# Residuals scaled and stored in the second mixer's opening, router tables first, and a page norm inside the pooling

## The reference, cut to what matters

```
for l in (0, 1):
    mixer = gated linear attention + SSD scan         if l == 0
            causal pooling + block-sparse attention   if l == 1     # paged K/V cache for the sample rows
    x = LayerNorm(alpha * x + mixer(x) @ w_out, ln_g[l, 0], ln_b[l, 0])      # alpha = 4 ** 0.25
    x = LayerNorm(alpha * x + experts(x),       ln_g[l, 1], ln_b[l, 1])      # 32 experts, 2 per row

def _layer_norm(x, g, b):
    return (x - mean(x)) * rsqrt(var(x) + LN_EPS) * g + b
def _pool_mix(u, buf, ...):   # s = sum of the last w rows, w = 2, 4, 8, 16 for four groups of 128 columns
    outs.append((s / cnt - u[..., lo:hi]) @ w_pool[group])
def _hier_moe(x, ...):        # router: 4 coarse + 32 fine logits of x; top group, then the top 2 experts of it
    ... silu(x @ w_gate) * (x @ w_up) * gate @ w_down
```

## Time and profile before

| what | value |
|---|---|
| median of 3 runs | 1218.51 us (1217.38 to 1221.27) |
| the profiled execution | 1223.9 us, its span 1222.1 us |
| PE busy | 1106.7 us (91%) |
| DVE busy | 501.2 us (41%) |
| ACT, POOL busy | 234.3 us (19%), 178.5 us (15%) |
| mean DMA rate over the span | 294 GB/s |

### The profile page before, as it was taken

How to read it: one execution, slowest core, us unless ns; L and a number is a source line. 1 busy time by engine, 2 the same in 40 slices (tenths; PEclk the granted TensorE clock), 3 DMA queues, 4 the chain that set the end, 5 groups by cost and what they waited for, 6 DMA issues and landing times. The chain is left out here.

```text
span 1222.1 us, 15209 instructions
## 1 busy us (share of the span) xinstructions
PE 1106.7 (91%) x5759; PEld 558.9 (46%) x5759; DVE 501.2 (41%) x1363; ACT 234.3 (19%) x519; POOL 178.5 (15%) x177
## 2 busy tenths in 40 slices
PE   8999999989999988876899999989899999788892
PEld 6874666655553333222543345544555433222330
DVE  3614666567642211111532314654787421111116
ACT  0311223321121100000421212333111211000003
POOL 0000000000011111100535532320000111111023
PEclk9999999999999999899999999989898999899895
DMA  7520210439489999996979979894895899999975
GB/s 289 191 97 4 78 67 1 147 119 422 179 309 408 420 420 420 420 421 249 394 281 328 381 264 365 299 363 174 325 378 199 319 408 419 419 421 421 421 284 222
DMA packets 85099, 358.84 MB, mean 294 GB/s; under 512 B 13959, under 2 KB 18188, under 8 KB 55324
## 3 DMA queue, kind: packets, MB, share of 16 engines
q1 hardware_dynamic: 63420, 279.57, 57.6%
q0 software_dynamic: 19520, 74.01, 15.7%
q10 hardware_dynamic: 2080, 4.19, 0.9%
HBM read 342.75 MB, written 31.16 MB: 306 GB/s over the span
## 5 line engine op out<-in xcount | busy, mean ns | idle before, releaser
L1896 PE MATMUL ahead_psum<-m_wg,top_xT 128*64 128x512 f32 x704 | 201.0, 633 | 33.2 <-DMA m_wg<-in_moe_w_gate_up 26.4
L1896 PEld LDWEIGHTS ahead_psum<-m_wg,top_xT 128*64 128x64 f32 x704 | 60.9, 145 | 145.9 <-issue 103.4
L1921 PE MATMUL n_psum_m<-m_wd,top_xT 128*64 128x512 f32 x456 | 121.1, 601 | 1.6 <-ACT top_xT L1979 1.0
L1896 PE MATMUL ahead_psum<-top_wide,top_xT 128*64 128x512 f32 x288 | 99.6, 624 | 12.5 <-DMA top_wide<-in_moe_w_gate_up 7.6
L1378 PE MATMUL ahead_psum<-top_wide,top_xT 128*128 128x512 f32 x224 | 103.0, 605 | 1.5 <-PEq L159 1.5
L1961 DVE COPY top_xT<-n_psum_t 128x512 f32<-128x512 f32 x31 | 21.4, 692 | 177.7 <-PE n_psum_t L1881 177.7
L2348 PE MATMUL ahead_psum<-top_wide,top_xT 128*128 128x512 f32 x192 | 86.0, 596 | 3.8 <-issue 3.3
L1816 POOL DMA_INDIRECT expert_rows<-e_Y,m_dest x33 | 32.9, 996 | 371.9 <-DVE e_Y L1970 334.2
L2152 POOL DMA_INDIRECT cd_kv<-in_cache_kT,top_kpages x64 | 61.0, 954 | 56.1 <-PE cd_psum_d L2391 32.4
L1378 PEld LDWEIGHTS ahead_psum<-top_wide,top_xT 128*128 128x128 f32 x224 | 41.1, 193 | 44.4 <-issue 44.3
L1921 PEld LDWEIGHTS n_psum_m<-m_wd,top_xT 128*64 128x64 f32 x456 | 35.3, 137 | 56.0 <-issue 53.2
(11 more groups left out here) (521 smaller groups left out, 1701.5 us busy)
## 6 DMA issues: line engine op xcount, KB each, us to landing
m_wg<-in_moe_w_gate_up SPq DMA_DIRECT2D x96, 1024.0 KB, 27.1
m_wd<-in_moe_w_down SPq DMA_DIRECT2D x56, 1024.0 KB, 26.8
top_wide<-in_moe_w_gate_up SPq DMA_DIRECT2D x32, 1024.0 KB, 20.3
cd_kv<-in_cache_kT SPq DMA_DIRECT2D x64, 256.0 KB
top_X<-in_moe_w_down SPq DMA_DIRECT2D x8, 1024.0 KB, 28.0
ab_w<-in_ab_w_in SPq DMA_DIRECT2D x2, 2048.0 KB, 11.2
top_wide<-in_ab_w_in SPq DMA_DIRECT2D x2, 2048.0 KB, 7.8
top_wide<-in_ab_w_out SPq DMA_DIRECT2D x2, 2048.0 KB, 8.9
```

The lines of the kernel that those rows point to most:

```text
L1896: last = nc.tensor.matmul(pg[i % 2][64 * a:64 * a + 64, :], xgT[i % 2][:, j, 64 * a:64 * a + 64], wg[E.slot(i, a)][:, j * 512:(j + 1) * 51 ...
L1921: last = nc.tensor.matmul(py[n2][64 * a:64 * a + 64, :], hT[:, j, 64 * a:64 * a + 64], wd[E.slot(i, a)][:, j * D + n2 * 512:j * D + (n2 + ...
```

## The change

1. In the second mixer's opening SP also loads gain and bias of `ln[0, 1]`, spread over 128 partitions, into the memory of the tile `vt`, between the expert rows and the weights of the projection. DVE's `restore(i)` stands there now, its five calls between `normal_scale(4)` and `copy_scores(1)`. SP stores each tile after its `restore` and no longer after ACT's norm. Its list is now: page group 0, tile 4, page group 1, tiles 0 and 1, group 2, tiles 2 and 3, group 3 and on. The memset of Q is moved behind `rotate("q", 0)`; the copy of the page scores waits for two stored tiles at group 0 and for the other two at group 4; ACT writes `vt` only after the last `restore`.
2. In the settling of l = 1 `restore` and its loads are gone. The router's three loads are the first that SP issues. DVE's list begins with the blanks and the tables. PE's `prepare()` stands between the two halves of tile 0 instead of behind a half of tile 1.
3. In the settling of l = 0 `prepare()` stands in the middle of the second half of `project(1, 1)`. In both layers `prepare_out()` is ahead of `add(1, 1)` on DVE.
4. In `window(3)` DVE runs `p_norm(7)` when sums of width 4 are made, instead of after the window and the copy of `newS`.

```diff
@@ settle_parts, sync
+        router()
         if back:
-            for i, (t, P) in enumerate(ORDER):
+            for t, P in ORDER:
                 sp.dma_start(X[:P, t, :], back(t)).then_inc(x_in[t], 16)
-                if i == 0:
-                    for p, got in ((slice(0, 32), old_in), (slice(32, 128), rest_in)):
-                        for a in range(2):
-                            sp.dma_start(E.xg[a][p, :], old[a].partition_broadcast(p.stop - p.start)).then_inc(got, 16)
-                        if got is old_in:
-                            router()
...
@@ settle_parts, tensor
             project(1, 0, second)
+            prepare()
             project(1, 1, second)
...
-            project(1, 1, second)
-        prepare()
+            project(1, 1, second[:2])
+            prepare()
+            project(1, 1, second[2:])
...
@@ settle_parts, vector
         if old:
-            restore(0)
+            blanks()
+            router_tables()
         add(0, 0)
         add(0, 1)
-        for z in (lg[:, :, :], As[:, :, :, :], A12[:, :, :], dif[:, :, :]):
-            c.add(V.memset(z, 0.0))
+        if not old:
+            blanks()
         spread_begin(0)
...
-        if old:
-            restore(1)
-            spread_end(0)
-            add(1, 0)
-        else:
-            add(1, 0)
-            spread_end(0)
+        if not old:
+            router_tables()
+        add(1, 0)
+        spread_end(0)
+        prepare_out()
         add(1, 1)
-        prepare_out()
         shift_of(0)
         for i in range(1, 5):
-            if old and i > 1:
-                restore(i)
             affine(i - 1)
...
@@ mixer_cd, sync
+            sp.dma_start(gamma, old[0].partition_broadcast(128)).then_inc(line_in, 16)
+            sp.dma_start(beta, old[1].partition_broadcast(128)).then_inc(line_in, 16)
             sp.dma_start(w[1][:, :, :], pieces[:, :, 1024:1536]).then_inc(w_in[1], 16)
...
             loads.k_plain(sp, 0)
-            for i, (t, P) in enumerate(ORDER):
-                sp.wait_ge(normed, i + 1)
-                sp.dma_start(kept[tok0(t):tok0(t) + P, :], X[:P, t, :]).then_inc(rows_stored if i else sample_stored, 16)
+            keep(0)
+            sp.wait_ge(normed, 5)
             loads.k_plain(sp, 1)
-            for n in (2, 3, 4, 5):
+            keep(1)
+            keep(2)
+            freed(2)
+            loads.k_plain(sp, 2)
+            keep(3)
+            keep(4)
+            for n in (3, 4, 5):
...
@@ mixer_cd, vector
+            def restore(i):
+                t, P = ORDER[i]
+                if i == 0:
+                    dve.wait_ge(line_in, 32)
+                dve.wait_ge(T_in, i + 1)
+                x = X[:P, t, :]
+                c.step(V.scalar_tensor_tensor(out=x, in0=x, scalar=ALPHA, in1=gamma[:P, :], op0=ALU.mult, op1=ALU.mult))
+                V.scalar_tensor_tensor(out=x, in0=beta[:P, :], scalar=ALPHA, in1=x, op0=ALU.mult, op1=ALU.add)\
+                 .then_inc(restored, 1)
...
-            window(3)
+            window(3, lambda: p_norm(7))
             V.tensor_copy(newS[:, :, :].rearrange("p g (b i) -> p g b i", b=NB), uS[:, :, :, NS:]).then_inc(ended, 1)
-            p_norm(7)
```

More of the change, by code:

```diff
@@ L2893, in window @@
                     width, i = 2 * width, 1 - i
+                    if width == 4 and between is not None:
+                        between()
                 inv = C("invcnt")[:, 16 * g:16 * g + PBUF]
@@ L2980, in _ @@
             rotate("q", 4)
+            restore(1)
             rotate("q", 0)
+            dve.wait_ge(sample_stored, 16)
+            c.add(V.memset(Q[:, :, :, :], 0.0))
             normal_copies(4)
+            restore(2)
             rotate("q", 1)
@@ L3001, in _ @@
             soften(0)
+            dve.wait_ge(rest_stored, 16 * 2)
             copy_scores(4)
@@ L3083, in build @@
                 ahead = [J.ps(f"{i}") for i in range(2)]
-                mixer_cd(nc, A, C, X, xT, pages, kpages, table, wide, [b[:, :] for b in ahead], between, yd, xs)
+                mixer_cd(nc, A, C, X, xT, pages, kpages, table, wide, [b[:, :] for b in ahead], between, yd, xs,
+                         (A["ln_g"][0, 1], A["ln_b"][0, 1]))
                 ahead.append(J.ps("2"))
```

55 lines of the change are left out of this document (26 added, 29 removed).

## The result

| | kernel before | changed kernel |
|---|---|---|
| median of 20 runs each | 1223.26 us (1217.38 to 1229.23) | 1215.80 us (1200.88 to 1222.95) |
| ratio | | 0.9912 (0.9891 to 0.9933) |
| the profiled execution: its time, its span | 1223.9, 1222.1 us | 1220.34, 1218.5 us |
| mean granted clock of it | 0.959 | 0.956 |

The ratio is 10.8 us off a kernel of 1223.3 (8.2 to 13.3). The two plain medians differ by 7.5 and the means of all 20 runs by 8.0 only, because they hold eight runs of the changed kernel over 1218.8 us that the ratio leaves out (it leaves out none of the kernel before), and the profiled execution is one of these: its total says little, its places can be read. So this set alone supports a gain of 7.5 to 10.8 us.

A forecast was written before the change was run, and what follows sets the result against it. PE, busy 91%, was taken as the bound, with the weight stream in the experts' stages and DVE where PE waits; 1.3 + 3.5 + 6.2 - 0 = 11.0 us off 1218.51 gave 1207.5, said as 1208, range 1203 to 1214.5.

The forecast's parts named there:

- Start of the first settling: Layer 0's settling: PE's 1.62 us wait for prepare_out before the first score goes; gain 1.3 us, bounds 0 to 1.6.
- DVE follows: First settling: DVE's next chain is loose, with a wait of 0.61 us for ACT alone, so DVE keeps up.
- Pooling: PE's 2.27 us wait for p_norm(7) and the 1.2 GHz clock after it go; gain 3.5 us, bounds 1.2 to 4.5.
- both new waits: Pooling: PE idle some 1.1 us before p_score(9) and 0.4 us before it turns step 8.
- Second settling: Layer 1's settling: the flip of tile 2's second half comes 6.2 us sooner, carried to the end; bounds 3.0 to 8.0.
- The opening: Second mixer's opening: five restores, 12.2 us of DVE, fit idle time; cost 0, bounds 0 to 2.5 us lost.
- The scores that I feared for: Opening: page scores at 631.21 and 668.63 us might wait for Q or pages; 3.9 and 5 to 6 us slack.
- Rival 1: Pooling and second settling: the clock falls at PE's new waits, costing 2.3 and about 3.2 us; 1211.5 us, chance 0.22.
- Rival 2: Layer 1's experts: the weight stream absorbs the second settling's 6.2 us; 1213.7 us, chance 0.09.

The follow-up runs named there:

- the second set: The changed kernel timed again without any edit, on another occasion, against the kernel before: ratio 0.9927, 8.9 us.
- filler: The changed kernel with six idle products on PE in the opening, before the second half of the q projection; ratio 0.9939 to the kernel before.
- no_first: The changed kernel with the first settling as in the kernel before; ratio 0.9919 to the kernel before.
- Order_only: The kernel before with the second settling's new order of loads, tables and small product, the five restores staying there; ratio 1.0054.
- combined: The changed kernel with the old first settling and, in the second, tile 1's gain and bias behind add(2, 1); ratio 0.9903 to the kernel before.
- second_only: The changed kernel with the first settling and the place of p_norm(7) as in the kernel before; ratio 0.9917 to the kernel before.

## Why the prediction was right, step by step

The sign and the size were right: 11.0 us forecast, 10.8 measured by the ratio (7.5 between the plain medians, 8.9 in the second set). The parts were not all of the size given. What belongs to the program at full clock is 1.4 + 0.7 + 6.7 = 8.8 us, 2.2 less than forecast. The rest of the 10.8 is not shown to be the program's, so that 11.0 and 10.8 lie this near each other by luck.

- **Start of the first settling, 1.3.** Right at its place: 1.54 at the first score. That it reaches the end is not shown. The step "DVE follows" ended the argument too soon: up to the second mixer no gain is seen (+0.4, standard error 1.0, which doesn't rule the 1.3 out). With no low clock at 330 us the stretch from the settling's start to the first expert's product is shorter by 1.37 (79.03 in filler, 80.40 in no_first, one trace each), so the gain stands in the program up to there; the seven traces with the edit had 4.4 us of low clock there on average and the seven without 2.2, which takes it all back. Whether the edit causes this is not shown.
- **Pooling, 3.5.** The mechanism and both new waits were right, the size was not. The sentence that from 808 to 810 PE had a clock of 0.50 "after it had stood idle" made one execution's fall a property of the wait. It fell at this wait in three of five traces with the old place, and in two of nine with the new one, behind the two short waits. The fixed part is 0.66 us, the mean over traces 1.5. So of the 3.5 us 2.8 were one execution's clock, and this is the term that was most mis-sized.
- **Second settling, 6.2.** Right: 6.5 at the flip, in every trace to 0.1 us, and a wait of 1.5 there for the 2.0 forecast. Carried on one to one: 6.7 at the last flip; the 8.3 at the first expert's product hold 1.6 of low clock. Order_only shows why it had to be summed over DVE's work up to the flip and not read off the first wait: the wait of 4.79 alone comes back as one of 5.02. In the means over traces this term was undersized by 2.1, about what the pooling was oversized by (2.0): that the two cancel is chance.
- **The opening, 0.** Right as far as the traces resolve it: 48 to 55 us to the page scores with the restores, 50.4 without their work, 49.7 to 51.6 in the old program. The scores that I feared for, of groups 0 and 3, did not wait for DVE or for pages. That all issuers' transfers share the same 16 engines (the Trainium skill, "DMA: Bandwidth & Descriptors", "Issuing engines are not separate DMA queues") had no price here: no page score waited for the stores' sake. That stores slow the loads beside them was the prediction's own inference from it; no run here shows it.
- **Rival 1, the clock at the new waits.** None of the six traces has a fall behind the flip's 1.53 us; two of nine have one in the pooling. The rule of the Trainium skill ("TensorE: Matmul & The Clock Gate", "HAM oscillation — how this bites in real kernels") that waits between bursts cost the clock is borne out only as a chance: the same 2.27 us of wait had 1.2 GHz behind it in some executions and 2.4 GHz in others. The page's example is a loop whose waits are longer than the bursts between them, which PE's new waits are not, so the prediction's "By this rule the time is rival 1's" asked more of the page than it says.
- **Rival 2, the gain absorbed in the experts' stage.** Not seen: from the first expert's product of layer 1 to the end it took 271.1 us with the change and 271.2 without (standard error of the difference 0.7).
- **What no step had:** the first mixer, 2.4 us longer in the kernels with the restores in the opening, though no edit touches it; 2.1 of this are the fall at 134 us.

## What to carry to other kernels

A wait that one edit removes is worth what is left when the next wait of the same engine chain is counted: sum the waiting engine's and the supplier's work up to the next place where they meet. Take a stage's length from several executions before a stretch of slow clock is priced as the consequence of a wait; here one trace turned 0.66 us into 3.5. Work that sits on a chain can be moved to a stage where its engine is idle anyway; here 12.2 us of it cost nothing there that the traces show.

## What the runs showed of the hardware

- Most of the spread between executions of one program goes with TensorE's clock. Over the 20 runs of the changed kernel time and mean granted clock have a correlation of -0.89, and 1.33 us go with 0.001 of clock; in the 84 runs of the kernel before beside the experiments -0.83 and 1.36. A mean lower by 0.001 over 1220 us is 2.4 us at half clock, and so 1.2 us of lost products: about what the slope says.
- The clock also falls where PE is busy throughout. The fall at 134 to 142 us came in seven of the nine traces of kernels with the restores in the second mixer's opening, 450 us later, and in none of the five without; it was absent in filler and combined. It makes 2.1 of the 2.4 us by which their first mixers are longer. What decides it stays open.
- ACT was late at one instruction, the copy of the first q tile, in thirteen of the fourteen traces: 1.1 to 3.4 us after its product had ended, mostly with no releaser in the trace. PE stood for 0.8 to 3.1 us for it in twelve. It is late too with PE kept busy (filler), and it was on time in second_only (0.04 us), where PE did not stand. Its cause stays open.
